# 128-column pieces at two tiles of the experts' second matrix, and other start addresses for the split weights

## The reference

```python
s = einsum('mhpd,hpnd->mhpn', q, sub_keys)         # 8 heads, 2 x 128 keys
...                                                # top 16 of 16 x 16 sums, g = softmax(top)
act = gelu(einsum('mhkd,md->mhk', expert_u[idx], xb))
w = g * act
return einsum('mhk,mhkd->md', w, expert_v[idx])    # the second matrix
```

## Time and profile before

| | |
|---|---|
| median of three runs | 2181.82 us (2180.7 to 2182.76) |
| the profiled execution | 2189.19 us, of which the span in the trace is 2187.4 |
| TensorE busy | 2109.6 us, 96% of the span |
| mean granted TensorE clock | 0.979 |
| first matrix (with the quads) | about 1403 to 1819 us |
| second matrix | 1821 to 2183 us |

### The profile page before, as it was taken

The page is one execution under the profiler, slowest core; times in us unless marked ns, Lnnn a source line. Parts: engine busy times, 40 slices in busy tenths (PEclk is TensorE's granted clock), DMA queues, the critical chain, the costliest instruction groups (busy, mean ns, idle before and its releaser), DMA issues.

```text
span 2187.4 us, 42620 instructions
## 1 busy us (share of the span) xinstructions
PE 2109.6 (96%) x18050; PEld 2003.8 (92%) x18050; DVE 1441.2 (66%) x2728; ACT 1087.9 (50%) x1881; POOL 481.7 (22%) x226
## 2 busy tenths in 40 slices
PE   7999999999999999999899988999999999999999
PEld 5977999999998789998678888999999999999999
DVE  4445478787784666766653656589388896666666
ACT  5333353232335455556433545555677776555554
POOL 1201100000012220002111441288766661000000
PEclk9999999999998999999889999999999999999999
DMA  7335345466663346653221235556544445555554
GB/s 268 111 136 183 116 154 183 165 241 229 211 224 117 111 158 209 219 189 132 77 68 59 77 126 167 171 186 196 167 138 146 152 140 181 189 186 185 188 187 145
DMA packets 97566, 354.90 MB, mean 162 GB/s; under 512 B 10720, under 2 KB 11744, under 8 KB 96992
## 3 DMA queue, kind: packets, MB, share of 16 engines
q1 hardware_dynamic: 97376, 352.18, 48.2%
HBM read 351.09 MB, written 1.05 MB: 161 GB/s over the span
## 4 chain that ended last, share of the span: by engine, by line
PE 86%; DVE 5%; ACT 3%; issue 3%; DMA 2%; POOL 2%; SPq 0%; POOLq 0%; DVEq 0%; ACTq 0%
PE ps L79 82%; PE ps L84 3%; PE ps L106 1%; ACT TH L157 1%; POOL TL L113 1%; DVE TL L113 1%; ACT SQ L154 1%; DMA RAW<-in_wada 1%; ACT Hh L157 1%; DVE ps L113 0%; POOL SM L113 0%; DMA AW<-in_wada 0%; DMA RAW<-in_wdn 0%; DMA RAW<-in_wup 0%; DVE SQ L113 0%
## 5 line engine op out<-in xcount | busy, mean ns | idle before, releaser
L157 ACT ACTIVATE TH<-RAW 128x1024 fp32r<-128x1024 f32 (+1 forms) x515 | 539.8, 1049 | 289.3 <-PE ps L79 260.7
L113 DVE TENSOR_TENSOR TL<-RAW,TH 128x1024 fp32r<-128x1024 f32 (+1 forms) x343 | 422.7, 1233 | 248.9 <-ACT TH L157 248.5
L113 POOL TENSOR_TENSOR TL<-RAW,TH 128x1024 fp32r<-128x1024 f32 x172 | 414.5, 2412 | 506.7 <-ACT TH L157 480.6
L79 PE MATMUL ps<-Hh,TL 128*128 128x256 f32 x1920 | 451.5, 288 | 15.6 <-DVE TL L113 6.3
L79 PE MATMUL ps<-Hh,TH 128*128 128x256 f32 x1920 | 439.6, 281 | 0.0
L79 PE MATMUL ps<-Hl,TH 128*128 128x256 f32 x1920 | 439.6, 281 | 0.0
L79 PE MATMUL ps<-HXh,TL 128*128 128x256 f32 x1314 | 366.0, 283 | 6.9 <-POOL TL L113 3.1
L79 PEld LDWEIGHTS ps<-Hh,TL 128*128 128x128 f32 x1920 | 323.1, 192 | 41.8 <-issue 18.5
L79 PE MATMUL ps<-HXh,TH 128*128 128x256 f32 x1314 | 360.2, 278 | 0.0
L79 PE MATMUL ps<-HXl,TH 128*128 128x256 f32 x1314 | 359.7, 278 | 0.0
L79 PEld LDWEIGHTS ps<-Hh,TH 128*128 128x128 f32 x1920 | 323.9, 192 | 0.7 <-issue 0.5
(11 more groups left out here) (338 smaller groups left out, 3128.3 us busy)
## 6 DMA issues: line engine op xcount, KB each, us to landing
RAW<-in_ut SPq DMA_DIRECT2D x128, 512.0 KB, 3.3
RAW<-in_v SPq DMA_DIRECT2D x128, 512.0 KB, 3.3
RAW<-in_wup SPq DMA_DIRECT2D x88, 512.0 KB, 4.3
AV<-in_wada SPq DMA_DIRECT2D x80, 512.0 KB, 3.9
RAW<-in_win SPq DMA_DIRECT2D x74, 512.0 KB, 3.8
RAW<-in_wada SPq DMA_DIRECT2D x56, 512.0 KB, 3.7
RAW<-in_wdn SPq DMA_DIRECT2D x32, 512.0 KB, 4.3
RAW<-in_wout SPq DMA_DIRECT2D x24, 512.0 KB, 3.8
```

Of the source, the lines that this page charges most:

```text
L79: return self.e.matmul(out, lhs, rhs, start=first, stop=last, skip_group_check=skip)
L113: return DRY if self.e is None else self.e.tensor_tensor(out, a, b, op)
L157: return DRY if self.e is None else self.e.activation(out, a, ACT.Copy, **kw)
```

## The change

At tiles 1 and 30 of the second matrix the products into bank 0 are taken as four pieces of 128 columns in place of two of 256, for each of the three pairs of parts. PAD0 moves ahead of TH and TL, so that these start at 64 modulo 512, as HXh to P still do. PAD1 grows from 8 to 15 floats. By the rounding to 32 bytes this moves AROW and all that is declared behind it by 32 bytes: what started at 64 modulo 512 starts at 96.

```diff
     RAW = sb("RAW", NRAW * TILE)
+    sb("PAD0", 112)
     TH = sb("TH", NSPLIT * TILE, F32R)
     TL = sb("TL", NSPLIT * TILE, F32R)
-    sb("PAD0", 112)
     HXh = sb("HXh", 2048, F32R)
...
     SM = sb("SM", 88)
-    sb("PAD1", 8)
+    sb("PAD1", 15)
     AROW = [sb(f"AROW{i}", 128) for i in range(2)]
...
             pe.wait_ge(*((D, "act_low", a) if l else (A, "act_high", a)))
-            for k in range(2):
-                at = 512 * (i % 2) + 256 * k
-                last = pe.mm(yb[i][:, 256 * k:256 * k + 256], e.WP[a % 3][l][:, c], r(w)[:, at:at + 256],
+            n = 128 if i == 0 and a in (1, 30) else 256
+            for k in range(0, 512, n):
+                at = 512 * (i % 2) + k
+                last = pe.mm(yb[i][:, k:k + n], e.WP[a % 3][l][:, c], r(w)[:, at:at + n],
                              a == 0 and z == 0 and k == 0, a == 127 and z == 2, True)
```

## The result

The changed kernel takes 2216.35 us (median of four runs, 2215.8 to 2223.85) against 2182.29 us before (2180.7 to 2190.15). The ratio is 1.0157, with a 95% interval of 1.0124 to 1.0189: slower by some 34 us, where 12 us less were forecast. The two profiled executions, 2189.19 and 2216.48 us, are 27.3 us apart, and so are their spans; that of before lies 7 us above its median. They also differ in the mean granted clock, 0.979 before and 0.984 after.

A forecast was written before the change was run, and what follows sets the result against it. PE was taken to bound the kernel. Profiled 2189.19 us less 13.5 gained plus 1.4 for the pieces gave 2177.1; carried to the median, 2181.82 - 12.1 = 2169.7 us, range 2166 to 2184.

The forecast's parts named there:

- What bounds the kernel: Whole kernel: PE, busy 96% of the span, sets the time; no wait in the second matrix is PE's.
- So the pace is a state that the instruction stream falls into and keeps, not a price of the operands.: Wide products: 113.3 or 117.8 ns with the same operands and code; the second matrix stayed slow for all 3,072.
- the 62 exits: First matrix: after 62 of 64 groups of 128-column products (quads), wide products go quick; used as evidence for the pieces.
- rival (a): Second matrix: pieces don't move the state, or it falls back at once; only cost left, 2183.3 us; chance 0.14.
- What the pieces may give: Second matrix, tiles 2 to 127: 3,024 wide products at 113.3 in place of 117.8 ns, 13.5 us gained.
- What the pieces cost: Second matrix, tiles 1 and 30: 12 more products and weight loads, 1.4 us; bounds 1.3 and 1.5.
- Addresses: "I take nothing": Moved start addresses: cost unknown, taken as nothing; bound 13 us either way from products on Hh and Hl.
- (c): Layers' products on Hh and Hl, and second matrix: starting at 96 modulo 512 holds products slow; 2196 us, chance 0.06.
- (d): Nearly all wide products: starting at 64 favours the quick pace everywhere, another 13 us, 2157 us; chance 0.04.
- The figures of N/2.4 + 2.5: Warm product starts: the skill's formula gives 109 ns for 256 columns, 56 for 128; 12 pieces would cost next to nothing.
- What would show it wrong: Second matrix: windows behind tile 1 still holding 852 instructions, or its start moving from 1821.4 by more than 2 us, among others.

The follow-up runs named there:

- e7: Kernel before with TH and TL moved to 0 modulo 512 by 96 of PAD0's floats ahead of them, all else as before; ratio 1.0063.
- e1: Kernel before with the pieces at tiles 1 and 30 of the second matrix alone, all addresses as before; ratio 0.9999.
- e5: Kernel before with 32 floats declared ahead of W, moving it from 64 to 192 modulo 512, no pieces in the second matrix; ratio 0.9936.
- e11: Changed kernel without its pieces, both paddings kept; ratio to before 1.0153.
- e6: Kernel before with W moved from 64 to 192 modulo 512 and the pieces at tiles 1 and 30 of the second matrix; ratio 0.9937.
- e2: Kernel before with PAD0 moved ahead of TH and TL alone, no pieces in the second matrix; ratio 1.0251, 2244.9 us.
- e4: Kernel before with 16 floats declared ahead of RAW, raising every start by 64 bytes and keeping all distances; ratio 0.9979.
- e8: Kernel before with TH and TL at 320 modulo 512, 256 bytes from all else; ratio 1.0266.
- e10: Kernel before with TH and TL at 160 modulo 512; ratio 1.0186.

## Why the prediction was wrong

- **What bounds the kernel.** Right, and it still holds: in every trace the second matrix ran at PE's own pace, without a wait of PE.
- **"So the pace is a state that the instruction stream falls into and keeps, not a price of the operands."** This is the step that failed, in its second half, and with it the use of the 62 exits. It rested on both paces occurring with the same operands and took from it that operands don't matter, which doesn't follow. The stretches of the earlier trace rows that it names for this, 240 to 258 and 880 to 930 us, don't even have the same operands: the first multiplies l0MIXl, HXh and HXl, the second Hh, Hl and l1midh, l1midl. What they share is the distance. All the quick stretches, in the earlier trace rows alike, had the moving operand 64 bytes below the stationary; the only stage at the other sign, the second matrix, was never seen quick. The prediction noted that under rival (a) as a point for it, and gave (a) 0.14.
- **What the runs showed in its place.** The distance of the two starts sets which paces there are and which one an exit mostly leads to: 62 of 64 exits behind quads quick at -64, none of 64 at +64 (e7), the second matrix slow at +64 with pieces (e1) and quick at -64 without (e5), and 116.7 to 120.0 ns at the other distances.
- **What the pieces may give.** 13.5 us were forecast, nothing came (e1). The 62 exits of 64 were evidence for distance -64 only. That e5 got 13.6 us shows that the two paces and the count of products were read rightly; it came by the distance, not by the change forecast.
- **What the pieces cost.** 1.4 us forecast; 1.3, 1.2 and 1.3 measured (e1, e11, e6).
- **Addresses: "I take nothing".** Measured 33 us (e11), beyond the 13 either way that I had set as the bound. That bound counted only products on Hh and Hl, half of them, and knew only two paces; the first matrix, of whose wide products only the stationary side moved, gave 15.9 of e11's 33.4 us.
- **The rivals.** (c) had the sign right, but its place half: it made 96 modulo 512 the culprit and left out the first matrix, at 64 and 64, the worst of all. (d), with 64 as the good start, is the opposite of e2.
- **The figures of N/2.4 + 2.5.** The prediction took N/2.4 + 2.5 ns from "Back-to-back issue gap" of the Trainium skill's "TensorE: Matmul & The Clock Gate" and left out that the section means a product by itself there and gives 81 ns at 128 columns and 131 at 512 for a stream of pairs of weight load and product. The streams here are such pairs: 113.3 ns or more at 256 columns, and 0.11 us at 128, above the 81. No term of the sum used the formula.
- **What would show it wrong** did: the second matrix starts 24.4 us later, at 1845.8, and e1's stage shows no quick product behind tile 1.

How the loss comes together, by the table: first matrix from -64 to 0, 113.6 to 119.6 ns on average; layers from -64 with its two paces (about 115 on average) to +32, 116.9; second matrix from +64 to -32, 117.8 to 118.3.

Left open: what in the memory or in PE makes the distance count, and why a break leads to one pace or the other. No run measures the two reads apart. Distances other than multiples of 32 bytes weren't tried, since the layout rounds to 32, and of 256 only one repetition was.

## What to carry to other kernels

When TensorE sets the time and every product loads new weights, look at the distance between two starts against what the shape should cost, and at where both operands begin relative to each other; moving one tensor by 128 bytes was worth 0.6% here (e5), and moving two by 448 cost 2.5% (e2). A pattern seen in many places is evidence only for the conditions that all these places share: list those conditions, and check whether the place to be changed has them. An edit that is only a padding gets its own experiment.

## What the runs showed of the hardware

- TensorE's start-to-start time for fp32r products of 128x128 with 256 columns, a weight load each, depends on the distance of its two operands' addresses, with its sign: 113.3 to 120.0 ns at a granted clock of 1.00 (table above). 0 and 256 bytes are alike. Shifting both by 64 bytes leaves the paces as they are (e4), and -64 was quick at three different places, 64 and 128, 128 and 192 (e5), 0 and 64 (e7).
- The Trainium skill ("SBUF — State Buffer", "Who interferes with whom") gives TensorE two independent read ports, one for the moving operand and one for weight loads, and says that it waits on no one. The runs speak against the two being independent in effect: the distance between what they read moves the time by up to 6%. Its section "Operand start alignment" makes a start a matter of legality and names no cost; here the starts of two tensors were worth 2.5% of the kernel (e2).
- At -64 and +64 the same code has two paces, 113.3 and 117.8 ns, and breaks in the stream switch between them. At -64 exits from quads ended quick 62 times in 64 (before), at +64 slow 63 times in 64 (e7).
- Beside e1 to e4 the kernel before ran from 2179.3 to 2194.1 us in 19 executions; the four each of e2 and e8, which have no stretch at the quick pace, lay within 2.3 us. That the two paces are why is argued, not shown, and they aren't the only cause: e10 has no quick stretch either, and its four executions go from 2221.05 us at a granted clock of 0.985 to 2232.81 at 0.975.
